# A hybrid encoder step on one core: 56 tiles of the input projection as three fp32r products instead of one fp32 product

## What is computed

```python
h = rmsnorm(x)                       # 544 x 2048
qkv, z, b_raw, a_raw, dq, dk, dv, gate_a, gate_b = split(h @ w_in)
o_a = gdn_branch(qkv, z, ...)        # gated delta rule: 9 blocks of 64 tokens, one after the other
o_b = diff_branch(dq, dk, dv, ...)   # differential attention: 8 heads, two maps each
merged = sigmoid(gate_a) * (o_a @ w_branch_a) + sigmoid(gate_b) * (o_b @ w_branch_b)
x = x + merged @ w_out               # then cross-attention, then PEER experts
```

## Time and profile before

| | us |
|---|---|
| median of three runs | 5595.38 |
| the profiled execution | 5596.68 |
| its span, first to last instruction | 5595.1 |
| memory projections and tiles of `qkv`, `z` (to the first fill unit) | 0 to 647 |
| recurrence with 1152 fill units | 647 to 1559 |
| attention with 640 fill units | 1559 to 1959 |
| merge, output, cross-attention | 1959 to 2850 |
| PEER experts and final norm | 2850 to 5595 |

### The profile page before, as it was taken

How to read it: one execution, slowest core, us unless ns; L and a number is a source line. 1 busy time by engine, 2 the same in 40 slices (tenths; PEclk the granted TensorE clock), 3 DMA queues, 4 the chain that set the end, 5 groups by cost and what they waited for, 6 DMA issues and landing times.

```text
span 5595.1 us, 78740 instructions
## 1 busy us (share of the span) xinstructions
PE 5437.0 (97%) x33527; PEld 5079.5 (91%) x33527; DVE 2963.2 (53%) x4099; ACT 1534.5 (27%) x1709; POOL 560.1 (10%) x534
## 2 busy tenths in 40 slices
PE   7999999999989999999989999999999999999998
PEld 6999988888867799997989999999999899999997
DVE  5455423223234443322259978887554566666665
ACT  4444311111123332213222234443223222222222
POOL 0000000000000000000000012322221211111110
PEclk9999999999999999999999999999999999999999
DMA  5422312222132243222232258887776877777773
GB/s 222 154 101 100 103 55 69 62 61 62 57 105 96 81 164 107 83 87 87 88 122 99 99 185 318 306 309 304 279 282 211 304 265 276 265 275 267 275 273 137
DMA packets 257490, 950.33 MB, mean 170 GB/s; under 512 B 46464, under 2 KB 130560, under 8 KB 179456
## 3 DMA queue, kind: packets, MB, share of 16 engines
q1 hardware_dynamic: 181792, 552.11, 28.5%
q0 software_dynamic: 59360, 379.63, 17.8%
q10 hardware_dynamic: 16128, 15.60, 0.8%
HBM read 855.84 MB, written 91.43 MB: 169 GB/s over the span
## 4 chain that ended last, share of the span: by engine, by line
PE 87%; DVE 8%; DVEq 2%; issue 1%; ACT 1%; DMA 1%; ACTq 0%; POOL 0%; SPq 0%; POOLq 0%; PEldq 0%
PE psum L1122 18%; PE psum L1197 18%; PE psum L845 16%; PE psum L1012 10%; PE psum L820 7%; PE psum L1029 3%; DVE e_lo L1917 2%; PE psum L796 2%; PE psum L1161 2%; PE psum L781 1%; PE psum L891 1%; PE psum L897 1%; PE psum L900 1%; DVEq L2129 1%; DMA ring<-in_v 1%
## 5 line engine op out<-in xcount | busy, mean ns | idle before, releaser
L845 PE MATMUL psum<-H,ring 128*128 128x272 f32 x3584 | 898.7, 404 | 0.7 <-ACT arena L1325 0.7
L1917 DVE TENSOR_TENSOR e_lo<-ring,e_hi 128x2048 fp32r<-128x2048 f32 x270 | 618.7, 2292 | 460.6 <-ACT e_hi L1437 444.6
L845 PEld LDWEIGHTS psum<-H,ring 128*128 128x128 f32 x3584 | 672.9, 193 | 164.9 <-issue 30.0
L1437 ACT ACTIVATE e_hi<-ring 128x2048 fp32r<-128x2048 f32 x270 | 517.4, 1916 | 927.3 <-PE psum L1197 770.3
L1197 PE MATMUL psum<-c_hi,e_hi 128*128 128x416 f32 x2048 | 722.3, 353 | 34.5 <-DVE e_lo L1917 24.9
L1122 PE MATMUL psum<-h_hi,e_hi 128*128 128x416 f32 x2032 | 719.1, 354 | 5.2 <-DVE e_lo L1917 5.2
L1197 PE MATMUL psum<-c_hi,e_lo 128*128 128x416 f32 x2048 | 724.0, 354 | 0.0
L1122 PE MATMUL psum<-h_hi,e_lo 128*128 128x416 f32 x2048 | 722.0, 353 | 0.0
L1197 PE MATMUL psum<-c_lo,e_hi 128*128 128x416 f32 x2048 | 716.1, 350 | 0.0
L1122 PE MATMUL psum<-h_lo,e_hi 128*128 128x416 f32 x2032 | 710.8, 350 | 0.0
L1197 PEld LDWEIGHTS psum<-c_hi,e_hi 128*128 128x128 f32 x2048 | 385.0, 188 | 48.5 <-issue 28.3
(11 more groups left out here) (421 smaller groups left out, 8846.1 us busy)
## 6 DMA issues: line engine op xcount, KB each, us to landing
ring<-in_weights SPq DMA_DIRECT2D x200, 1024.0 KB, 4.8
ring<-in_uT SPq DMA_DIRECT2D x128, 1024.0 KB, 5.2
ring<-in_v SPq DMA_DIRECT2D x128, 1024.0 KB, 6.9
hid<-tmp POOLq DMA_DIRECT2D x128, 208.0 KB, 6.3
gates<-arena POOLq DMA_DIRECT2D x13, 2048.0 KB, 9.5
arena<-hid SPq DMA_DIRECT2D x32, 832.0 KB, 9.7
arena<-gates SPq DMA_DIRECT2D x32, 832.0 KB, 12.6
gate_in<-arena ACTq DMA_DIRECT2D x64, 136.0 KB, 3.0
```

The source lines that it names most:

```text
L845: mm = nc.tensor.matmul(psum[:, b, 0:HN], ring[:, tile % R, k * P:(k + 1) * P], H[:, k, b * HN:(b + 1) * HN], start=(k == 0), stop=(k == K ...
L1437: nc.scalar.activation(hi_slot(n, reg), e_raw[n % R], ACT.Copy).then_inc(w_rounded, 1)
L1917: nc.vector.tensor_tensor(e_lo[n % R], e_raw[n % R], as_f32(hi_slot(n, reg)), ALU.subtract)\
```

## The change

The fill's units become three fp32r matmuls each, from `p_hi` and `p_lo`, which stay where they are, and from hi and lo parts of the weight tile. So ACT rounds and DVE splits each of the 56 tiles: the rounding of tile n + 2 stands behind the evacuation of tile n's second half, on ACT; the split stands at fixed places of DVE's program, four in each block of the recurrence and behind the group of queries that comes at least twelve units before the tile is used in the attention (`split_tiles`; DVE's loop over heads is written out for this). `H` is no longer read by the fill, so the arrays of recurrence and attention (and the hi parts, `f_hi`) move into its place, where `p_hi` and `p_lo` would have been overwritten. There are two staging slots instead of four. The last head no longer prepares the merge's tiles, since the tiles go on in the same sequence; and ACT rounds `OA` only after the last head's norm, as the target lies in `H`.

```diff
-F_TILE, F_HALF, F_SLOTS = 2 * KD, KD, 4
+F_TILE, F_HALF, F_SLOTS = 2 * KD, KD, 2
...
+UNITS_AT = [ATT_UNITS * h + ATT_FILL["vt"] + sum(ATT_FILL["a"][0:q]) + sum(ATT_FILL["aT"][0:q])
+            for h in range(HEADS) for q in range(QT)] + [ATT_UNITS * HEADS]
+F_GDN = 4 * (NCH + 1)
...
+        f_hi = [placed(f"f_hi{b}", AT_H + AT_FILL_HI + b * D, [D]) for b in range(2)]
         def hi_of(n):
-            return w_first[n % 2] if n < W_MERGE else w_hi[n % 2]
+            return w_first[n % 2] if n < T_FILL else f_hi[n % 2] if n <= T_FILL + F_GDN else w_hi[n % 2]
...
             rows_of(0)
             pool.dma_start(ndist, t["ndist"]).then_inc(at["dist_in"], 16)
+            cache_of(0)
+            pool.wait_ge(fill_full, 2 * (F_GDN + 1))
             pool.dma_start(ndist_s[0:NS, :], t["ndist_s"]).then_inc(at["dist_in"], 16)
-            cache_of(0)
             rows_of(1)
...
                     if u % F_TILE == 0:
-                        pe.wait_ge(w_full[tile % R], 16 * (tile // R + 1))
+                        pe.wait_ge(w_split, tile + 1)
...
-                    mm = nc.tensor.matmul(psum[:, b, 0:HN], ring[:, tile % R, k * P:(k + 1) * P],
-                                          H[:, k, b * HN:(b + 1) * HN], start=(k == 0), stop=(k == KD - 1))
+                    cols, tok = slice(k * P, (k + 1) * P), slice(b * HN, (b + 1) * HN)
+                    w = hi_of(tile)[:, cols], e_lo[tile % R][:, cols]
+                    for n, (a, x) in enumerate(((w[0], p_hi), (w[0], p_lo), (w[1], p_hi))):
+                        mm = nc.tensor.matmul(psum[:, b, 0:HN], a, x[:, k, tok],
+                                              start=(k == 0 and n == 0), stop=(k == KD - 1 and n == 2))
...
                     act.dma_start(dst, fst[:, slot, :]).then_inc(fill_out[slot], 16)
+                    if b == 1 and n != F_GDN - 1:
+                        round_w(T_FILL + n + 2)
...
-                    if h == HEADS - 1 and 2 <= q < 4:
-                        round_w(W_MERGE + q - 2)
...
             act.wait_ge(fill_full, 2 * N_FILL)
+            act.wait_ge(at["done"], HEADS)
             for k in range(HEADS):
                 round_src(oa_hi, OA, S_OAB, k)
-            act.wait_ge(at["done"], HEADS)
...
                                         over_heads(cst("upper", CH)), ALU.mult).then_inc(s["d_gu"], 1)
+                if c:
+                    split_w(T_FILL + 4 * c + 1)
...
                     .then_inc(s["d_r"], 1)
+                split_w(T_FILL + 4 * c + 2)
                 for lv in range(1, LEVELS):
...
                     dve.drain().then_inc(s["d_r"], 1)
+                    if lv == 2:
+                        split_w(T_FILL + 4 * c + 3)
...
                     .then_inc(s["d_rr"], 1)
+                split_w(T_FILL + 4 * c + 4)
...
+            def split_tiles(h, q):
+                for k in range(1, N_FILL - F_GDN + 1):
+                    if UNITS_AT[QT * h + q] <= F_TILE * k - 12 < UNITS_AT[QT * h + q + 1]:
+                        split_w(T_FILL + F_GDN + k)
...
-                    if last and q >= 3:
-                        split_w(W_MERGE + q - 3)
+                    split_tiles(h, q)
...
             head_norm(HEADS - 1)
+            split_w(T_MERGE + 1)
```

More of the change, by code:

```diff
@@ L291, in program @@
                                                       sem("ba_done"), sem("ba_in"))
[L295 to L299, removed]
+        flat_H = H[:, :, :].rearrange("p a b -> p (a b)")
+        chunk = [view(flat_H, 3 * HEADS * CH * b, 3 * HEADS, CH)[0] for b in range(2)]
+        Sp, e = view(flat_H, 2 * 3 * HEADS * CH, HEADS, DH)
+        AT_FILL_HI = 4 * NP_ + 3 * NT + NP_
+        assert e <= AT_FILL_HI and AT_FILL_HI + 2 * D <= KD * NT
+        fst, e = view(tmp, TMP_N - 2 * HN, F_SLOTS, HN)
+        assert e <= TMP_N
         e = BIG + HEADS * NPAD
@@ L334, in program @@
         e = 0
[L335 to L344, removed]
+        ndist, e = view(flat_H, e, 4, NP_)
+        kc, e = view(flat_H, e, 1, NP_)
+        early, e = view(flat_H, e, 3, NT)
+        assert e <= AT_FILL_HI
+        late, e = view(flat_H, AT_FILL_HI, 3, NT)
+        ndist_s, e = view(flat_H, e, 1, NT)
+        rows = [early, late]
+        vc, e = view(flat_H, e, 4, DH)
+        sc, e = view(flat_H, e, 2, NT)
+        pr, e = view(flat_H, e, 1, NT)
         assert e <= KD * NT
@@ L1232, in round_w @@
             def round_w(n, reg=None):
-                tile = tile_of(n)
+                tile = n
                 act.wait_ge(w_full[tile % R], upto(16 * (tile // R + 1), reg, 16))
-                if n >= 2:
+                if 2 <= n < T_FILL + 2:
                     act.wait_ge(tile_done, upto(n - 1, reg, 4))
+                elif T_FILL + 2 <= n < T_MERGE + 2:
+                    act.wait_ge(fill_full, 2 * (n - 1 - T_FILL))
+                elif n >= T_MERGE + 2:
+                    act.wait_ge(tile_done, done(n - 2))
                 nc.scalar.activation(hi_of(n), ring[:, tile % R, :], ACT.Copy).then_inc(w_rounded, 1)
@@ L1304, in first_rows @@
                     act.drain().then_inc(raw_ready, 1)
-                    if not (last and j == 2):
-                        round_w(T_GDN + (4 * i if last else 0) + j + 2, None if last else i)
+                    round_w(T_GDN + (4 * i if last else 0) + j + 2, None if last else i)
                     act.wait_ge(conv_done, i * 3 + (j + 1))
@@ L1325, in first_rows @@
                 nc.scalar.activation(z, acc[1], ACT.Silu).then_inc(acc_free, 1)
-                if not last:
-                    round_w(T_GDN + 5, i)
+                round_w(T_GDN + (4 * i if last else 0) + 5, None if last else i)
             with act.Fori(0, HEADS - 1) as i:
@@ L1388, in _ @@
             act.wait_ge(outs, 48)
+            round_w(T_FILL + F_GDN + 1)
             for h in range(HEADS):
@@ L1609, in split_w @@
             def split_w(n, reg=None):
[L1610 removed]
+                slot = n % R
                 dve.wait_ge(w_rounded, upto(n + 1, reg, 4))
@@ L1688, in first_rows @@
                     dve.drain().then_inc(conv_done, 1)
-                    if not (last and j == 2):
-                        split_w(at_w + j + 2, reg)
+                    split_w(at_w + j + 2, reg)
                 dve.wait_ge(qk_root, i + 1)
@@ L1698, in first_rows @@
                 dve.drain().then_inc(qk_done, 1)
-                if not last:
-                    split_w(at_w + 5, reg)
+                split_w(at_w + 5, reg)
             with dve.Fori(0, HEADS - 1) as i:
@@ L1799, in attention_head @@
                     rows = P if q < 4 else NS
+                    if h == 0 and q == 4:
+                        dve.wait_ge(at["dist_in"], 32)
                     for m in range(2):
@@ L1824, in attention_head @@
                                                    op0=ALU.mult, op1=ALU.add).then_inc(at["a"], 1)
-                    if q == 0 and not first:
+                    if q == 0 and h:
                         head_norm(h - 1)
-                    if last and q >= 3:
-                        split_w(W_MERGE + q - 3)
-            attention_head(0, True, False)
-            with dve.Fori(1, HEADS - 1) as h:
-                attention_head(h, False, False)
-            attention_head(HEADS - 1, False, True)
+                    split_tiles(h, q)
+            for h in range(HEADS):
+                attention_head(h)
             head_norm(HEADS - 1)
+            split_w(T_MERGE + 1)
             def split_src(lo, src, hi, k, n):
```

12 lines of the change are left out of this document (4 added, 8 removed).

## The result

The changed kernel takes **5504.25 us** (median of four runs, 5501.56 to 5513.14) beside 5594.62 for the kernel before (four runs, 5592.36 to 5595.81): a ratio of 0.9842, 95% interval 0.9825 to 0.9859. Forecast were 5480 and a range of 5450 to 5545. The profiled execution took 5501.56 with a span of 5500.0, so 95.1 us are gone between the two profiles, where the sum promised 116.

The account below looks back on a forecast made before the run. The prediction took PE (TensorE), with 87% of the span, as the bound, its gains limited by spare time at waits. Profiled 5596.7 - 108 (recurrence) - 12 (attention) + 4 (merge) = 5480.7, about 5480 us as median; range 5450 to 5545.

Parts of the forecast that it names:

- the mechanism that the forecast rested on: At each PE wait: a fill piece shortened by more than its spare time turns the rest into waiting.
- The pace of a unit: Fill: a unit falls from 0.466 to 0.376 us, saving 0.090: 103.7 us in the recurrence, 57.6 in the attention.
- The 4 us expected on top at half clock: Recurrence, last four units of each block: at half clock they save 0.20 us each instead of 0.09.
- rule of four passes: Fill: three fp32r products would take 3/4 of one fp32 product, 0.350 us a unit; the prediction used measured rows instead.
- The attention: Eight heads: 23 us gained after waits, less 11 for the new roundings, so -12 us.
- rival D: Attention: new waits in the heads bring the clock down to 1.2 GHz; slower, 5676 us; chance 0.06.
- Rival F: Heads, set against e1_hold: fp32r products or transfers, not waits, pull the clock down; 5485 us; no chance given.
- The merge: Ahead of the merge's first product: a rounding (1.92) and a split (2.29) are added, +4 us.
- Rival A: Whole fill: all of the pace counts and the attention loses nothing to waits; 5433 us; chance 0.06.
- Rival B: Recurrence: DVE's splits reach its path; 82 us go back, 5562 us, or 5521 with two of four; chance 0.12.
- Rival C: Fill: fp32r products between small fp32 ones run no faster than one fp32 product; 5610 us, slower; chance 0.06.

Follow-up runs that it names:

- second profile: The changed kernel run and profiled once more with no edit; 5510.65 us, 0.9843 of the kernel before.
- e1_hold: Changed kernel, with 8 of the attention's 20 ScalarE roundings held until the copy TensorE waits for is issued; 5503.78 us.
- e1_hold2: e1_hold with its own two new waits taken out: held roundings wait for the next exponentials, no split behind head_norm; 5499.25 us.
- e4_twice: Changed kernel with the cost of the recurrence's roundings and splits doubled, on 34 tiles; 5549.80 us.
- e2_both: e1_hold's edit on the changed kernel, plus 9 fill units per head moved from the recurrence to the attention; 5475.15 us.
- e3_cover: e2_both plus 28 fill units at the attention's start, where TensorE waits for the first head's rows; 5478.42 us.
- e6_best: e3_cover with e1_hold2's edits, ScalarE's evacuations of the 28 leading units ahead of its state-transfer wait, and 2 units of aT3 moved; 5473.07 us.
- e8_four: Changed kernel with a fourth product, low weights by low tokens, in the attention's 640 units alone; 5545.13 us.
- e7_order: e6_best with the 28 leading units ahead of TensorE's wait for the recurrence's last output, and head_norm never beside a split; 5456.17 us.
- e7_merge: e7_order with the recurrence output's roundings and splits moved ahead of the last head's norm, TensorE's wait for it mid-tile; 5453.68 us.

## Why the prediction was right, and where its terms were off

**The sign and the range** held, and so did the mechanism that the forecast rested on: no new wait of PE at `d_gu`, `d_a`, `d_r` or `d_rr`, and waits at every step of a head. The size was off by some 21 us of 116, in two terms. One of the signs that were named for being wrong was there too: a granted clock of 0.50 within the heads.

**The pace of a unit** was mis-sized. The step "12.11 / 26 = 0.466" took a mean over a whole piece, and set beside it 0.376 from a run without ends. The ends of a piece cost something in both kernels. The changed kernel, PE and its weight loads at the start of the 26-unit piece, and PE at its end:

```profile
837.50 1.12 PE L887 MATMUL psum<-tmp,const 64*128 64x512 f32 x2
838.55 0.19 PEld L854 LDWEIGHTS psum<-p_hi,f_hi 128*128 128x128 f32 x1 [0.76 <-issue]
838.55 0.39 PE L854 MATMUL psum<-p_hi,f_hi 128*128 128x272 f32 x1
838.65 0.19 PEld L854 LDWEIGHTS psum<-p_lo,f_hi 128*128 128x128 f32 x1
838.78 0.29 PE L854 MATMUL psum<-p_lo,f_hi 128*128 128x272 f32 x1
...
848.30 0.29 PE L854 MATMUL psum<-p_hi,e_lo 128*128 128x272 f32 x1
848.52 0.68 PE L893 MATMUL psum<-const,tmp 64*64 64x64 f32 x8
```

From the second product to the last, 76 steps take 9.52 us, 0.1253 each: 0.376 a unit, as forecast. But the first product holds PE for 0.23 and the last for 0.22, some 0.2 us more per piece. The first weight load starts together with its product, where the second one starts 0.13 ahead of its own. The Trainium skill (TensorE: Matmul & The Clock Gate, Architectural detail: the array is 16× 32×32, not 1× 128×128) says that PE's queue can pull a weight load ahead of products in flight; inside a piece the trace agrees, at the first product of this one it does not.

The kernel before has the same ends: a 7-unit piece runs from here to 890.45, 3.40 us.

```profile
887.05 3.48 PE L845 MATMUL psum<-H,ring 128*128 128x272 f32 x14
```

So a unit without ends is (12.11 - 3.40) / 19 = 0.458, and the difference 0.082, not 0.090: 94.5 us in the recurrence instead of 103.7, and 52.5 in the attention instead of 57.6. Measured, the fill's pieces in the recurrence fell from 569.8 to 475.2 us, by 94.6. The 4 us expected on top at half clock came out as nothing, for a reason that the prediction left out. The last four units of a block gave back what it says; the changed kernel's, beside the 3.79 us of the earlier trace rows:

```profile
818.24 0.59 PE L854 MATMUL psum<-p_hi,f_hi 128*128 128x272 f32 x1
...
821.13 1.41 PE L938 MATMUL psum<-tmp,const 128*128 128x512 f32 x2
```

That is 2.89 us, 0.9 less. But the time at half clock did not shrink with the work: 85.3 us in the recurrence before and after (95.6 in the second profile), so it reaches further into the next pieces and takes the gain back there.

The Trainium skill's rule of four passes for true fp32 (FP8 and Floating Point Precision, TensorE Precision Notes), weighed in the prediction, is a little farther off still than it seemed: 0.376 / 0.458 is 0.82, where the estimate from that rule was 0.75.

**The attention**, -12 forecast and +0.6 measured. The waits themselves came out smaller than forecast: 40.3 against 8.1 before, 32 us, where 4.3 a head and 11 for the roundings made 45. Step by step: q = 2, 3 and 4 wait 0.4, 0.5 and 0.9 (forecast 0.5, 0.7, 0.9), `vt` 1.9 three times (1.8); q = 1 waits 0.3, not 1.6; `aT` of q = 0 waits 2.3 four times, where 0.8 stood. Against these 13 us to the good stand 5 us of pace, some 7 us that are left over (perhaps the ends of pieces, whose last product no longer overlaps anything where PE waits; they were not measured apart), and **14 us by the clock**, a term that the forecast put at nothing. That the misses cancel in part is luck. Why q = 1 waits so little is open. The clock's part is rival D's mechanism, at less than a tenth of its price: the waits brought the clock down, for 3.4 or 6.8 us at a time and not for the rest of the stage. The evidence that the prediction set against it, a window with one 0.78 us wait at full clock, was true and too small: it showed one wait, not the five to seven of a head.

Waits (the length of the stage less PE's busy time) and clock over the kernels, in the eight heads:

| kernel | units | heads, us | waits, us | at half clock (falls that begin there), us |
|---|---|---|---|---|
| before | 640 | 399.5 | 8.1 | 0 |
| changed, two profiles | 640 | 400.1, 404.1 | 40.3, 39.9 | 30.7, 41.0 |
| e1_hold, e1_hold2 | 640 | 399.4, 395.0 | 43.7, 36.8 | 27.3, 27.3 |
| e4_twice | 640 | 399.2 | 41.2 | 23.9 |
| e2_both, e3_cover, e6_best | 712, 720, 720 | 400.6, 402.1, 396.0 | 22.9, 25.6, 20.0 | 13.7, 6.8, 10.2 |
| e8_four | 640 of four products | 439.5 | 18.3 | 3.4 |
| e7_order, e7_merge | 720, 720 | 384.7, 386.3 | 12.4, 12.5 | 0, 3.4 |

Rival F of e1_hold is out: e7_order runs the same fp32r products, more of them, with the same transfers, at full clock. That waits set the falls off in the heads is shown from both sides, here and by the added falls of e4_twice; e7_merge's one fall stands right behind its 2.0 us of waiting for head 0's rows. Waits are not all that does: at the end of every block of the recurrence the clock falls in every kernel of the table, where PE waits for nothing. What decides after a given wait is open: in the changed kernel's first profile the three of 1.9 us before `vt` were each followed by a fall, of the four of 2.3 us two, of the eight of about 0.9 three; and of e8_four's four waits of 2.0 us one.

**The merge**: +4 forecast, 4.2 measured, by the two instructions named. **Rival A** (all of the pace counts, 5433) fails as argued; PE's busy share is 96% of the span, 97% before, and the Trainium skill's advice to work on the most contended engine (Perfetto Trace Analysis, Identifying the Most-Contended Engine) carried in the recurrence alone; in the heads it did not, as e8_four shows. **Rival B** (VectorE's splits on the path) fails: no wait. But the forecast costed the splits at nothing by VectorE's idle time and by a tile's whole length of cover for PE, and of this cover one split in each block had 0.8 us left (e4_twice). No row of the prediction shows that; the prediction was lucky here. **Rival C** (fp32r no faster) fails: products start 0.125 us apart.

**What was overlooked**: a wait of 1.8 us for the first chunk at the start of the recurrence. The load of the chunk and PE's first product with it, before and after:

```profile
653.12 2.76 SPq L545 DMA_DIRECT2D arena<-qkv x2
658.80 1.04 PE L865 MATMUL psum<-const,arena 128*64 128x128 f32 x8
```

```profile
650.04 2.96 SPq L550 DMA_DIRECT2D H<-qkv x2
655.58 1.03 PE L874 MATMUL psum<-const,H 128*64 128x128 f32 x8 [1.82 <-DMA H<-qkv]
```

The load starts 5.8 and 6.0 us after the fill's first product, in both kernels when the same transfer has landed, so the move of the arrays doesn't hold it up. But the 24 units ahead of PE's first product are 2 us cheaper, and PE comes before the data. It is the prediction's own mechanism at a place where it read no spare time; e2_both, with four units fewer there, waits 3.6 us.

## What to carry to other kernels

Price a unit of work from the difference between a long and a short stretch of it, in both kernels; a mean over one piece holds its ends too. When work that covers a chain gets cheaper, the gain stands where the cover is thick (the recurrence) and turns into waits where it is thin (the heads); then move work from the one to the other, which gave 28.6 us here (e2_both beside e1_hold), and 48 together with the other changes of order in e7_order. And look at the granted clock behind new waits of TensorE: they can cost more than their length, as in e4_twice.

## What the runs showed of the hardware

- TensorE's granted clock fell to half, for 3.4 or 6.8 us at a time, behind waits of 0.9 to 2.3 us in the changed kernel's heads: eight falls, with 40.3 us of waits in 400. With 12.4 us of waits in 384.7 (e7_order) it did not fall in the heads. In e4_twice 13.6 us of waits in the recurrence cost some 24 to 32 us more by the clock. At half clock the fill's products start 0.226 us apart instead of 0.125.
- Without any wait it falls at the end of every block of the recurrence: 85.3 us at half clock there before and after the change.
- The first product of a piece behind the recurrence's small products holds PE 0.1 us longer than the next ones, with its weight load starting together with it, and the last one 0.09 longer. In fp32 the two ends together cost the same 0.2 us (3.40 us for 7 units of 0.458). An fp32r product of 64 columns set between others costs 0.113 us, an fp32 one 0.23; the change of type itself showed no price.
- Three fp32r products of 272 columns take 0.376 us, one fp32 product 0.458.
